# A fused encoder layer on eight cores: prologue loads, projections and output products in another order

## The reference

```python
def _layer(x, pool_hist, pos0, norm1_g, w_in, pool_w, pool_scale, gmlp_ws, gmlp_b,
           w_out, norm2_g, w_up, w_down):
    h = _rmsnorm(x, norm1_g)
    z = h @ w_in                                                         # (B,T,IN_WIDTH)
    a = z[..., :POOL_WIDTH]
    u = jax.nn.gelu(z[..., POOL_WIDTH:POOL_WIDTH + GMLP_WIDTH])
    v = jax.nn.gelu(z[..., POOL_WIDTH + GMLP_WIDTH:])
    pool_out, new_hist = _pool_mixer(a, pool_hist, pos0, pool_w, pool_scale)
    gmlp_out = _gmlp_gate(u, v, gmlp_ws, gmlp_b)
    x = x + jnp.concatenate([pool_out, gmlp_out], axis=-1) @ w_out
    f = _rmsnorm(x, norm2_g) @ w_up
    x = x + jnp.square(jax.nn.relu(f)) @ w_down
    return x, new_hist, v
```

## Time and profile before

| | us |
|---|---|
| median of 3 runs (lowest, highest) | 1244.65 (1243.24, 1247.44) |
| the profiled execution, its own time | 1243.03 |
| span of its slowest core, core 2 | 1241.4 |
| spans of the 8 cores | 1238.2 to 1241.4 |
| DVE, ACT, POOL busy on core 2 | 497.0, 377.6, 114.5 |

### The profile page before, as it was taken

One profiled execution on the slowest core, in us unless ns is written; L12 is line 12 of the kernel. 1 busy time (PEld: TensorE's weight loads), 2 busy tenths in 40 slices (PEclk: granted clock), 3 DMA queues, 4 the chain that ended last, 5 costly groups with the idle time before them and its releaser, 6 DMA issues.

```text
span 1241.4 us, 19257 instructions; the slowest of 8 cores (1238.2 to 1241.4 us)
## 1 busy us (share of the span) xinstructions
PE 1229.8 (99%) x6863; PEld 654.4 (53%) x6863; DVE 497.0 (40%) x915; ACT 377.6 (30%) x737; POOL 114.5 (9%) x193
## 2 busy tenths in 40 slices
PE   8999999999999999999999999999999999999998
PEld 4555545555545544554555455455545545554554
DVE  5654434454534432442443254334425423450313
ACT  5452312135313330331233043223304322420422
POOL 5621000001011010100001010000101010000000
PEclk9999999999999999999999999999999999999999
DMA  9999978559459538746953784586378449747752
GB/s 184 185 240 190 225 171 208 136 128 314 161 152 270 176 135 235 222 167 160 276 192 136 219 239 170 163 244 210 131 216 258 170 145 246 135 165 229 253 206 85
DMA packets 90543, 240.52 MB, mean 194 GB/s; under 512 B 57201, under 2 KB 57329, under 8 KB 67666
## 3 DMA queue, kind: packets, MB, share of 16 engines
q1 hardware_dynamic: 77328, 187.08, 49.0%
q0 software_dynamic: 12944, 51.88, 19.2%
q10 hardware_dynamic: 178, 0.33, 0.1%
HBM read 214.47 MB, written 34.43 MB: 201 GB/s over the span
## 4 chain that ended last, share of the span: by engine, by line
PE 95%; DMA 4%; POOL 0%; issue 0%; ACT 0%; DVE 0%; ACTq 0%; DVEq 0%; POOLq 0%
PE ps L738 30%; PE ps L807 28%; PE ps L622 9%; PE ps L449 8%; PE ps L700 7%; PE ps L720 7%; PE ps L485 4%; DMA WOUT<-w_out 2%; PE ps L829 2%; DMA WAU<-w_au 1%; PE ps L574 1%; PE ps L370 0%; DMA X<-xall 0%; POOL WAU L300 0%; PE ps L605 0%
## 5 line engine op out<-in xcount | busy, mean ns | idle before, releaser
L738 PE MATMUL ps<-H2T,RING 128*128 128x384 bf16 x2304 | 384.4, 326 | 1.0 <-ACT ST L742 1.0
L807 PE MATMUL ps<-RING,ST 128*128 128x512 bf16 x1632 | 353.7, 379 | 0.0
L738 PEld LDWEIGHTS ps<-H2T,RING 128*128 128x128 bf16 x2304 | 223.8, 98 | 148.5 <-issue 2.0
L807 PEld LDWEIGHTS ps<-RING,ST 128*128 128x128 bf16 x1632 | 159.7, 98 | 191.7
L318 ACT ACTIVATE JUNK<-X 128x1024 bf16<-128x1024 f32 (+1 forms) x102 | 105.0, 1030 | 433.8 <-DVE X L814 290.0
L742 ACT ACTIVATE ST<-ps 128x384 bf16<-128x384 f32 x288 | 140.3, 489 | 208.6 <-PE ps L738 208.5
L744 DVE TENSOR_TENSOR ST<-ST 128x384 bf16<-128x384 bf16 x288 | 96.7, 356 | 192.4 <-ACT ST L742 192.1
L814 DVE TENSOR_TENSOR X<-ps,X 128x512 f32<-128x512 f32 x48 | 33.2, 692 | 216.2 <-PE ps L807 216.2
L449 PE MATMUL ps<-HT,WAU 128*128 128x384 bf16 x640 | 106.3, 326 | 1.9 <-DMA WAU<-w_au 1.3
L449 PEld LDWEIGHTS ps<-HT,WAU 128*128 128x128 bf16 x640 | 62.2, 98 | 43.6 <-issue 3.1
L720 PE MATMUL ps<-RING,ST 128*128 128x512 bf16 x384 | 83.7, 379 | 0.0
(11 more groups left out here) (126 smaller groups left out, 747.4 us busy)
## 6 DMA issues: line engine op xcount, KB each, us to landing
RING<-scr SPq DMA_DIRECT2D x144, 1024.0 KB, 5.7
RING<-w_mlp POOLq DMA_DIRECT2D x16, 1024.0 KB, 22.4
scr<-RING SPq DMA_DIRECT2D x16, 1024.0 KB, 12.7
X<-xall POOLq DMA_DIRECT2D x27, 512.0 KB, 5.5
yall<-X POOLq DMA_DIRECT2D x27, 512.0 KB, 12.3
X<-xall SPq DMA_DIRECT2D x6, 512.0 KB, 9.7
yall<-X SPq DMA_DIRECT2D x5, 512.0 KB, 10.4
WAU<-w_au POOLq DMA_DIRECT2D x8, 256.0 KB, 12.0
```

Source lines behind the costliest of these rows:

```text
L738: i_ = e.matmul(bank(ub)[:, 0:TOK], lhsT=RING[s][:, k, (m % 4) * 128:(m % 4 + 1) * 128], rhs=H2T[:, k, :], start=(k == 0), stop=(k == 7))
L807: i_ = e.matmul(bank(n)[:, :], lhsT=ST[:, kg * 8 + kk, n * 128:(n + 1) * 128], rhs=RING[s][:, kk, :], start=(kg == 0 and kk == 0), stop=(k ...
```

## The change

Four places of the hand-written order change, and two helpers get options for it.

1. Loads: WAU piece 6 is issued ahead of tile 2 of step 1, and the two small loads (`INVC`, `PSC`) come after piece 7.
2. Prologue: one warm-up product fewer. The first piece's eight products are split: the first four use the blocks that VectorE copied, the other four wait for ScalarE's copy. The projections of tile 0 of step 1, the transposes and the pool mixer stand in another order; pieces 0 and 1 of step 1 are made tile by tile for tiles 1 and 2. The pool mixer's groups of step 0 go 0 and 2, then 1 and 3, and group 3 of step 1 goes from GpSimd to VectorE. The copy of 16 tokens to the next step (`gen_halo_next`) is apart and on VectorE.
3. Output products of steps 0 and 1: all products of half 0 first (but one), then the fold of half 1, then those of half 1.
4. Step 2: the three squares of step 3's norm stand one ahead of each of up products 14 to 16.

```diff
@@ -437,19 +437,23 @@
-        def gen_WI_au(i, m0=0, m1=8, n0=0, n1=NT):
+        def gen_WI_au(i, m0=0, m1=8, n0=0, n1=NT, split=False):
...
+                HTd = [("HTd", i, n) for n in range(n0, n1)]
+                halves = [(range(4, 8), B.HTk[n0:n1 - 1] + HTd), (range(4), B.HTk[n1 - 1:n1])] if split else \
+                    [(range(8), B.HTk[n0:n1] + HTd)]
+                for ks, rd in halves:
...
@@ -555,10 +559,13 @@
-            if i < NS - 1 and g1 == 4:
-                N = bufs(i + 1)
-                add(eng, lambda e: e.tensor_copy(out=N.A[:, :, 0:16], in_=B.A[:, :, TOK:TOK + 16]),
-                    reads=[B.Ak(g) for g in range(4)], writes=[N.Ahk(g) for g in range(4)])
+            if 1 < i < NS - 1:
+                gen_halo_next(i)
...
@@ -881,10 +888,10 @@
         load_wau(4)
         load_wau(5)
+        load_wau(6)
         gen_L(1, "pool", 2, 3)
+        load_wau(7)
         load_pool_parts()
-        load_wau(6)
-        load_wau(7)
...
@@ -897,7 +904,7 @@
         gen_N1_T(0, 1, 2)
-        gen_warm(2)
+        gen_warm(1)
         gen_N1_T(0, 2, 3, shared=True)
...
@@ -916,39 +923,47 @@
-        gen_WI_au(0, 0, 3)
+        gen_WI_au(0, 0, 1, split=True)
+        gen_WI_au(0, 1, 3)
         norm_T((HBH, DTall), HT, ("HT", NT), 0, 16)
-        gen_WI_au(0, 3, 4)
         gen_N1_T(1, 0, 1, shared=True)
-        gen_WI_halo()
...
+        gen_WI_au(0, 3, 4)
+        gen_halo_next(0)
         first_apply(1, 1)
+        gen_WI_halo()
         gen_WI_au(1, 0, 4, 0, 1)
         gen_PL(0, 0, 1)
-        gen_WI_au(0, 4, 5)
+        gen_PL(0, 2, 3)
+        gen_WI_au(0, 4, 6)
+        gen_WI_au(1, 4, 6, 0, 1)
         first_sq(1, 2)
         norm_rs("2", 2, 3)
         first_apply(1, 2)
-        gen_PL(0, 1, 4)
-        gen_WI_au(0, 5, 6)
-        gen_WI_au(1, 4, 6, 0, 1)
+        gen_N1_T(1, 1, 2)
         gen_WI_au(0, 6, 7)
-        gen_N1_T(1, 1, 2)
+        gen_WI_au(1, 6, 7, 0, 1)
         gen_WI_au(0, 7, 8)
         gen_N1_T(1, 2, 3)
-        gen_WI_au(1, 6, 8, 0, 1)
-        gen_WI_au(1, 0, 8, 1, 3)
+        gen_WI_au(1, 7, 8, 0, 1)
+        gen_WI_au(1, 0, 2, 1, 2)
+        gen_WI_au(1, 0, 2, 2, 3)
+        gen_WI_au(1, 2, 8, 1, 3)
+        gen_PL(0, 1, 2)
+        gen_PL(0, 3, 4)
...
-        gen_PL(1, eng="pool")
+        gen_PL(1, 0, 3, eng="pool")
+        gen_PL(1, 3, 4)
+        gen_halo_next(1)
...
@@ -956,31 +971,29 @@
-        gen_WI_v(1, 1, 2)
+        gen_WI_v(1, 1, 3)
         gen_fold(0)
-        gen_WI_v(1, 2, 3)
-        gen_fold(1)
         for k in range(4):
             p1[k]()
+        gen_WO_pe(0, hhs=(0,))
+        gen_WO_pe(1, n1=2, hhs=(0,))
+        gen_fold(1)
         for n in range(NT):
-            gen_WO_pe(0, squares=True, n0=n, n1=n + 1)
+            gen_WO_pe(0, squares=True, n0=n, n1=n + 1, hhs=(1,))
             norm_rs("2", n, n + 1)
         gen_N2_apply(0, 0)
-        gen_WO_pe(1, n1=1)
+        gen_WO_pe(1, n0=2, hhs=(0,))
         gen_N2_apply(0, 1)
-        gen_N2_apply(0, 2)
         gen_N2_T(0, 0, 1)
...
+        for n in range(NT):
+            gen_WO_pe(1, squares=True, n0=n, n1=n + 1, kind="f", hhs=(1,))
+            norm_rs("f", n, n + 1)
+            if n == 0:
+                gen_N2_apply(0, 2)
+            else:
+                gen_N2_apply(1, n - 1, "f")
+            if n < NT - 1:
+                gen_N2_T(0, n + 1, n + 2)
...
@@ -1046,9 +1059,12 @@
                 gen_UP(i, 4, 14)
-                gen_N1_elem(3)
+                for n in range(NT):
+                    norm_square("1", n, X[0][:, n, :], [("X", 0, n)])
+                    gen_UP(i, 14 + n, 15 + n)
+                gen_N1_elem(3, squares_done=True)
                 gen_L(4)
-                gen_UP(i, 14, 22)
+                gen_UP(i, 17, 22)
```

More of the change, by code:

```diff
@@ L424, in first_apply, with gen_N1_elem @@
             hbs.setdefault(("1", s), []).append(norm_apply("12"[s], n, X[s][:, n, :], [("X", s, n)], G1B, G1k))
-        def gen_N1_elem(i):
+        def gen_N1_elem(i, squares_done=False):
             b = i % NXB
             srcs = [(X[b][:, n, :], [("X", b, n)]) for n in range(NT)]
-            norm_stats("1", srcs)
+            norm_stats("1", srcs, squares_done=squares_done)
             hbs[("1", i)] = [norm_apply("1", n, X[b][:, n, :], [("X", b, n)], G1B, G1k) for n in range(NT)]
@@ L445, in gen_WI_au, with mm @@
                 fb = next_front()
[L447 to L452, removed]
+                HTd = [("HTd", i, n) for n in range(n0, n1)]
+                halves = [(range(4, 8), B.HTk[n0:n1 - 1] + HTd), (range(4), B.HTk[n1 - 1:n1])] if split else \
+                    [(range(8), B.HTk[n0:n1] + HTd)]
+                for ks, rd in halves:
+                    def mm(e, m=m, fb=fb, ks=ks):
+                        for k in ks:
+                            i_ = e.matmul(bank(fb)[:, c0:c1], lhsT=WAU[:, m, k, :], rhs=B.HT[:, k, B.ho + c0:B.ho + c1],
+                                          start=(k == halves[0][0][0]), stop=(k == halves[-1][0][-1]))
+                        return i_
+                    add("pe", mm, reads=rd + [("WAU", m)], writes=[("BANK", fb)])
                 if m < 4:
@@ L557, in gen_PL, with gen_halo_next @@
                         reads=["T16", ("A", g)], writes=[("DT", g)])
-            if i < NS - 1 and g1 == 4:
-                N = bufs(i + 1)
-                add(eng, lambda e: e.tensor_copy(out=N.A[:, :, 0:16], in_=B.A[:, :, TOK:TOK + 16]),
-                    reads=[B.Ak(g) for g in range(4)], writes=[N.Ahk(g) for g in range(4)])
+            if 1 < i < NS - 1:
+                gen_halo_next(i)
+        def gen_halo_next(i):
+            B, N = bufs(i), bufs(i + 1)
+            add("dve", lambda e: e.tensor_copy(out=N.A[:, :, 0:16], in_=B.A[:, :, TOK:TOK + 16]),
+                reads=[B.Ak(g) for g in range(4)], writes=[N.Ahk(g) for g in range(4)])
         def gen_PG_pieces(i):
```

## The result

| | before | after |
|---|---|---|
| median (lowest, highest), 6 runs each, us | 1244.04 (1243.24, 1247.44) | 1252.56 (1251.13, 1253.11) |
| profiled execution, us | 1243.03 | 1251.13 |
| slowest core, its span, us | core 2, 1241.4 | core 4, 1249.6 |

The changed kernel takes 1.0062 times as long (95% interval 1.0049 to 1.0076), or 7.7 us more. The ratio is worked out from all executions and not from the two medians, which lie 8.5 us apart. That is slower, inside the range, and 1.3 us above the forecast.

What follows compares the result with a forecast made beforehand. TensorE, busy 1229.8 of 1241.4 us, was taken as the bound. Terms 2.1 + 1.5 + 1.9 - 0.2 + 2.3 - 0.2 = +7.4 us gave 1250.4 (profiled) or 1252.1 (median), forecast 1251.3; range 1247.8 to 1254.8.

Steps and rivals of the forecast that it cites:

- Part 1: Loads and prologue: late INVC delays VectorE's scaled tile and TensorE's third transpose, so v starts 2.1 us later.
- the rival: Idleness before step 1's third transpose lowers TensorE's clock to half speed, costing 2.5 us (1253.8 us); chance 0.10.
- the rule by which it could overtake: Loads: completion is not first in, first out, so small INVC could land earlier and prologue cost come to about 0.
- Part 2: Output-stage folds: TensorE waits for ScalarE's copies of folded weights, +1.5 and +1.9 us; weight-load wait removed, -0.2 us.
- Part 3: Transposes of norm 2, output stage: waits of 0.8 at HB0, 0.3 at HB2, 1.2 at H2T copy; +2.3 us.
- Part 4: Step 2: squares no longer hold back ScalarE's bank copies; -0.2 us, bounds 0 and 1.0.
- The load is what is late next: Step 2: the new ring buffer's load lands 0.3 us before the product's old start, limiting the gain to 0.2 us.
- Group 3 of step 1 at no cost: Moving this pool-mixer group to VectorE costs nothing: about 3 us at 45 us, where VectorE was idle until 48.7.
- INVC in time: Rival: the small load lands before 28 us, so the prologue ends near -0.5 us, time 1248.7 us; chance 0.13.
- a shifted load: Rival: a load shifted some 7 us meets another in the first steps, adding 2 to 4 us (1254.5); chance 0.05.
- The output stage waits for nothing: Rival: folded blocks are back in time and 5.7 us of the sum go, time 1245.6 us; chance 0.10.
- The removed waits alone: Rival: the change gives what it removes and makes no wait, 3.1 us less (1241.5 us); chance 0.04.

Runs made afterwards that it cites:

- group 2 behind: Changed kernel with VectorE's pool-mixer group 2 of step 0 moved behind the scaled tile 2 of step 1; 1.0067 times the kernel before.
- changed, again: The changed kernel, unaltered, measured once more beside later runs on the same chip; 1250.95 us, 1.0070 times the kernel before.
- front only: Changed kernel with the output stage of the kernel before; 1246.23 us, 1.0028 times the kernel before.
- folds covered: Changed kernel with each fold one block of products earlier; 1.0054 times the kernel before.
- squares only: Kernel before with only the three squares of step 2 placed one per up product; 1242.57 us, 1.0001 times the kernel before.
- INVC early: Changed kernel with the two small loads, INVC and PSC, issued ahead of weight piece 6; 1247.78 us, 1.0040 times the kernel before.
- output, group 3 on VectorE: Kernel before with the changed output stage and with group 3 of step 1's pool mixer on VectorE; 1247.14 us, 1.0039 times the kernel before.
- output only: Kernel before with only the changed output stage; 1250.72 us, 1.0067 times the kernel before.
- group 2 behind, group 3 on GpSimd: Changed kernel with step 0's group 2 behind step 1's scaled tile 2, and step 1's group 3 back on GpSimd; 1247.14 us, 1.0038 times the kernel before.
- warm fill: Changed kernel with fourteen warm-up products ahead of step 1's third transpose; 1.0068 times the kernel before.

## Why the prediction was right, and where a size was off

**The sum.** In the profiles v starts 4.6 us later (45.94 against 41.32), from v to up it takes 4.9 us more (40.73 against 35.87), and from up to the end 1.3 us less (1162.9 against 1164.2): 8.2 us. The prediction had 2.1, 5.5 and -0.2, together 7.4. That the two sums are so near is partly luck: the clock added 2.8 us that the forecast didn't have, and its other terms were 2.0 us too large together (0.3, 0.6 and 1.1). The two cores compared are also the latest of their eight in each kernel: by the medians of the eight, v starts 3.6 us later (43.97 against 40.40).

**Part 1: the mechanism right, the rival on top.** The third transpose started at 35.17 on core 4, for 35.4 predicted. INVC's reader started at 29.89, for 30.5, and from there to the transpose it took 5.3 us instead of 4.9, so two small errors cancel in part. INVC landed behind the last WAU piece on all eight cores, so the rule by which it could overtake did nothing here; the Trainium skill (DMA: Bandwidth & Descriptors, HWDGE ordering) states that rule for hardware queues, and these loads went through the software queue, so this is no test of it. From the third transpose to v it took 10.77 us, and 8.0 on core 4 of group 2 behind, where the clock was 1.00 (32.00 to 40.00); 8.1 was predicted. So the clock took 2.8 of the 4.6 us, and 1.8 are left for the 2.1 of the forecast. What failed is a chance: "no idle time of the trace so far did" bring the clock down, so I gave the fall 0.10. Before, no idle time of that length stood in the middle of the work. It fell on 6 of 8 cores, then on 5 of 8 (changed, again), and on 5 of 8 in front only and in folds covered. The price that I gave it, 2.5 us, is near what the slowest core paid (2.8); on the other five cores it was 1.3 to 1.6 us. The Trainium skill (TensorE: Matmul & The Clock Gate, Part 1) says that the gate follows how busy the array was and then passes half of the pulses; the trace agrees with it, with 0.50 granted to an array that was fully busy again.

**Part 2: right.** The listed waits are 1.02 and 1.71 us, and the forecast had 1.5 and 1.9. But a wait costs more than its row: from the end of the work ahead to the start behind, 0.17 us is in no row (71.36 is 1.88 us behind 69.48, where the fold's four products of 0.216 us end), and the gate products start 0.3 us behind the fold besides. With these it is 1.5 and 1.9. No core waits for that load any more, as predicted; with the unlisted 0.17 this gives back 0.4 rather than 0.2.

**Part 3: right but for 0.4 us.** 0.48 at HB0 and 0.96 at the H2T copy, with 0.17 each and 0.12 at HB2: 1.9 us for 2.3. All three waits stood where they were predicted.

**Part 4: too small.** "The load is what is late next" failed as the rule for every core. On cores 1 and 2 nothing was late next (squares only), and the whole 1.0 us of core 2 came back. In the changed kernel core 7 alone waits 0.9 us for the ring's load. As it also matters which core is the slowest, this is worth between 0 and 1 us.

**Group 3 of step 1 at no cost: right in the changed kernel, but the cover was thinner than I had it.** I gave it about 3 us of VectorE, and on core 4 it took 5.2 (43.96 to 49.13). VectorE then stood idle for 4.2 us, because TensorE came to the gate late, by the wait and the clock of part 1. Where TensorE came earlier, it depended on when VectorE was done. With INVC early VectorE's list is earlier too, and seven of eight cores had no wait over 0.2 us for it; in output, group 3 on VectorE, five of eight; in group 2 behind, where INVC was still late, none, and the whole gain was given back. The move also had a worth that I didn't give it, but only beside the prologue of before (3.5 us, output only). Beside the new prologue TensorE didn't wait for GpSimd without it either (group 2 behind, group 3 on GpSimd). For the changed kernel itself I estimate the same: GpSimd is done with group 2 at 54.3 us on core 4, group 3 took it 7.9 us in that run, which makes 62.2, and the first reader comes at 65.2.

**The other rivals.** INVC in time was made by hand (INVC early) and gave 1.0040, where 1248.7 is 1.0032 times the 1244.65 shown before: right in size. Nor did a shifted load cost 2 to 4 us in the first steps: from up to the end the cores take 1162.7 to 1163.8 us, and before they took 1162.7 to 1164.2. The output stage waits for nothing: false in every run with that stage. The removed waits alone, as far as they could be had without new ones, gave 0.9995.

## What to carry to other kernels

Follow a moved load to its first reader and then down that reader's list: here a load of 32 KB held a small operation, and behind it stood the tile that the busiest engine needed. Count a wait of TensorE of about 3 us twice, for itself and for the clock behind it, since here the clock fell behind most of them and added 1.2 to 2.8 us. When a wait is removed or products are moved ahead, ask whose lateness that had covered: in group 2 behind VectorE took all of the gain, and in output only the earlier products met a GpSimd that was not done.

## What was unexpected of the hardware

- The clock came down behind several waits of about 1 us too (group 2 behind, 52 to 56 us, three waits, 0.67 over the next 5 us).
- VectorE's three f32 additions of 128x397 took 3.61 us in group 2 behind (the first VectorE row there), while GpSimd was at its own additions. In the changed kernel they took 1.91 us, while GpSimd was idle; VectorE, core 4:

```profile
37.70 1.91 DVE L535 TENSOR_TENSOR PQ<-PQ 128x397 f32<-128x397 f32 x3
```

  The Trainium skill (SBUF — State Buffer, SBUF: two separate sides) says that the two share a pair of ports, which one of them holds for a whole instruction; the trace agrees in that VectorE's three additions take 1.9 times as long beside GpSimd's.
- TensorE waited up to 2.4 us for "issue" at the first v product of warm fill. No run settles what that is.
